# Gated expert rows added to a per-token sum in DRAM, in place of a last stage that gathers them

## The reference

```python
h = layer_norm(ALPHA_RES * h + mix, ln1_g[l], ln1_b[l])            # h1
top_logit, top_e = lax.top_k(logits, TOP_K)                        # TOP_K = 4 of 32
gates = jax.nn.softmax(top_logit, axis=-1)
hu = lax.ragged_dot(xs, w_gate_up, group_sizes) + b_gate_up[e_sorted]
act = (up + 1.0) * gate * jax.nn.sigmoid(SWIGLU_ALPHA * gate)      # gate, up: clipped halves of hu
y = lax.ragged_dot(act, w_down, group_sizes) + b_down[e_sorted]
y = y * g_sorted[:, None].astype(y.dtype)
out = jnp.zeros_like(xf).at[tok].add(y)
h = layer_norm(ALPHA_RES * h + ffn, ln2_g[l], ln2_b[l])
```

## Time and profile before

| | |
|---|---|
| median of 3 runs | 4528.32 us (4526.23 to 4531.88) |
| profiled execution, span | 4529.3 us |
| PE / DVE / ACT / POOL busy | 4289.9 / 3076.1 / 1817.6 / 1010.1 us |
| PE share of the span | 95% |
| DMA | 665.72 MB, 147 GB/s over the span |
| HBM read / written | 543.61 / 120.03 MB |

### The profile page before, as it was taken

One profiled execution on the slowest core, in us unless ns is written; L12 is line 12 of the kernel. 1 busy time (PEld: TensorE's weight loads), 2 busy tenths in 40 slices (PEclk: granted clock), 3 DMA queues, 4 the chain that ended last, 5 costly groups with the idle time before them and its releaser, 6 DMA issues. The chain is left out here.

```text
span 4529.3 us, 70549 instructions
## 1 busy us (share of the span) xinstructions
PE 4289.9 (95%) x24356; PEld 3153.5 (70%) x24356; DVE 3076.1 (68%) x4861; ACT 1817.6 (40%) x2677; POOL 1010.1 (22%) x1152
## 2 busy tenths in 40 slices
PE   8999988999999998699999999999999999999987
PEld 4444434444444454599989889899999999999961
DVE  2587867878888873555556556666676777777768
ACT  1222223443434433233434444444445555555530
POOL 1111101221111122211112212222222222222235
PEclk9999989999999999799999999999999999999986
DMA  6443330120110010544555456474657667667668
GB/s 194 126 122 92 87 101 16 30 27 21 18 23 16 14 27 19 148 158 148 174 168 190 155 183 220 162 250 161 237 197 239 208 230 241 219 234 237 212 214 362
DMA packets 534140, 665.72 MB, mean 147 GB/s; under 512 B 64416, under 2 KB 402592, under 8 KB 533952
## 3 DMA queue, kind: packets, MB, share of 16 engines
q1 hardware_dynamic: 419664, 501.02, 34.7%
q10 hardware_dynamic: 87744, 77.15, 5.4%
q0 software_dynamic: 26576, 85.56, 5.0%
HBM read 543.61 MB, written 120.03 MB: 147 GB/s over the span
## 5 line engine op out<-in xcount | busy, mean ns | idle before, releaser
L2000 PE MATMUL gu<-x_hi,w_hi 128*128 128x240 f32 (+8 forms) x4096 | 1196.5, 292 | 4.1 <-issue 4.1
L2003 PE MATMUL gu<-x_lo,w_hi 128*128 128x240 f32 (+8 forms) x4096 | 1195.5, 292 | 0.5 <-issue 0.5
L2004 PE MATMUL gu<-x_hi,w_lo 128*128 128x240 f32 (+8 forms) x4096 | 1194.1, 292 | 0.0
L2106 DVE TENSOR_TENSOR w_lo<-w_raw,w_hi 128x2048 fp32r<-128x2048 f32 x386 | 874.6, 2287 | 414.1 <-ACT w_hi L2190 386.2
L2190 ACT ACTIVATE w_hi<-w_raw 128x2048 fp32r<-128x2048 f32 x386 | 726.8, 1908 | 207.4 <-PE gu L2004 132.0
L2000 PEld LDWEIGHTS gu<-x_hi,w_hi 128*128 128x128 f32 x4096 | 774.7, 189 | 4.5 <-issue 4.3
L2003 PEld LDWEIGHTS gu<-x_lo,w_hi 128*128 128x128 f32 x4096 | 773.3, 189 | 1.1 <-issue 0.9
L2004 PEld LDWEIGHTS gu<-x_hi,w_lo 128*128 128x128 f32 x4096 | 773.8, 189 | 0.0
L1972 POOL TENSOR_TENSOR a_lo<-up,a_hi 128x384 fp32r<-128x384 f32 x256 | 396.6, 1549 | 1177.8 <-ACT a_hi L2202 1177.8
L570 PE MATMUL proj_acc<-w_in_sb,hT 128*128 128x512 f32 (+1 forms) x1280 | 499.0, 537 | 0.7 <-ACT hT L586 0.7
L2000 PE MATMUL yp<-w_hi,a_hi 128*128 128x512 f32 x1088 | 445.6, 410 | 2.3
(11 more groups left out here) (316 smaller groups left out, 5878.6 us busy)
## 6 DMA issues: line engine op xcount, KB each, us to landing
w_raw<-w_gate_up SPq DMA_DIRECT2D x258, 1024.0 KB, 7.6
w_raw<-w_down SPq DMA_DIRECT2D x128, 1024.0 KB, 8.1
y_dram<-y_rows ACTq DMA_DIRECT2D x128, 256.0 KB, 2.6
y_dram<-zeros ACTq DMA_DIRECT2D x12, 2688.0 KB, 15.5
h_blk<-h_dram SPq DMA_DIRECT2D x32, 512.0 KB, 8.7
qi_dram<-qi_stage ACTq DMA_DIRECT2D x16, 640.0 KB, 3.2
x_in<-x SPq DMA_DIRECT2D x16, 512.0 KB, 6.1
w_in_sb<-w_in SPq DMA_DIRECT2D x4, 2048.0 KB, 14.2
```

The lines of the kernel that those rows point to most:

```text
L2000: op = nc.tensor.matmul(out, s_hi_, m_hi, start=(n == 0), stop=False)
L2003: nc.tensor.matmul(out, s_hi_, m_lo, start=False, stop=False)
L2004: op = nc.tensor.matmul(out, s_lo_, m_hi, start=False, stop=(n == len(pairs) - 1))
L2106: nc.vector.tensor_tensor(w_lo[:, c % 2, cols], raw[:, c % 3, cols], w_hi[:, c % 2, cols].bitcast(F32), ALU.subtract).then_inc(s_lo, 1)
```

## The change

1. A second array in DRAM, `sums`, begins as a copy of h1 (each block is stored twice), and h1 and `sums` get 512 spare rows, cleared to zero. ACT's zero stores into `y` go, and `y` with them.
2. A list entry is now a pair, token number and gate divided by ALPHA_RES (`entry`). Lists are cleared to (2048 + n, 0.0), so that an unused entry names a spare row.
3. In a visit ACT multiplies by the row's gate while it copies out of PSUM. POOL adds each of six tiles to the token's row of `sums` by an indirect DMA with an add (seven DMAs, tile 2 is two). `who` is copied to `who_held` first; `hold_places` and `hold_gates` make row numbers and gates of it behind j = 2 and 3. SP loads the list entries of row tile 2 in its packed form (`load_third`) ahead of the visit.
4. The last stage loads `sums`, adds the bias matmul and norms it, with epsilon divided by ALPHA_RES squared. ACT makes the sums of the rows and of their squares, POOL the scale, DVE three passes. Gathers, `g_sum`, relays of positions and gates go. Eight tiles are in flight.

The core of the diff (row numbers left out; the same names):

```diff
 # attend_stage, SP
-                sp.dma_start(D_["lists"][0:EXPERTS * SEQ, :].rearrange("(p n) o -> p (n o)", p=P),
-                             res[:, 0:EXPERTS * SEQ // P].bitcast(I32)).then_inc(s_clear, 16)
...
+                shape = [CLEARED, 2, 2 * ROWS]
+                sp.dma_start(D_["lists"].rearrange("(p a n) o -> p a (n o)", p=CLEARED, a=2),
+                             res[0:CLEARED, 0:2 * ROWS].bitcast(I32).unsqueeze(1).broadcast_to(shape)
+                             ).then_inc(s_clear, 16)
+                for name in ("h1", "sums"):
+                    sp.dma_start(D_[name][SEQ:, :].rearrange("(m p) n -> p m n", p=P),
+                                 res[:].unsqueeze(1).broadcast_to([P, 1 + ROWS // P, D])).then_inc(s_clear, 16)
...
-                    sp.dma_start(D_["h1"][b * P:(b + 1) * P, :], h1[:]).then_inc(s_h1st, 16)
+                    for name in ("h1", "sums"):
+                        sp.dma_start(D_[name][b * P:(b + 1) * P, :], h1[:]).then_inc(s_h1st, 16)
 # attend_stage, DVE, weigh
-                    nc.vector.tensor_copy(at_i[:], at_f).then_inc(s_at, 1)
+                    nc.vector.tensor_copy(at_i[:], at_f)
+                    nc.vector.tensor_copy(entry[:, :, 0], token[:, b:b + 1].broadcast_to([P, TOP_E]))
...
-                    nc.vector.tensor_scalar(S["gates"][:, b], e_gate, e_inv, None, ALU.mult).then_inc(s_gate, 1)
+                    nc.vector.tensor_scalar(entry[:, :, 1].bitcast(F32), e_gate, e_inv, 1.0 / ALPHA_RES,
+                                            ALU.mult, ALU.mult).then_inc(s_at, 1)
+                    nc.vector.tensor_scalar(S["gates"][:, b], e_gate, e_inv, 1.0 / ALPHA_RES, ALU.mult, ALU.mult
+                                            ).then_inc(s_gate, 1)
 # experts_stage, SP
+                def load_third(v):
...
+                    if not first(v):
+                        sp.wait_ge(s_hold, v)
+                    for i in range(4):
...
+                        sp.dma_start(third[i * FEW:(i + 1) * FEW], D_["lists"][bass.ds(row, FEW), :]
+                                     ).then_inc(s_third, 16)
+                    sp.dma_start(spot[:], A["spots"][bass.ds(rest + few, 1)].rearrange("o p j n -> (o p) j n")
+                                 ).then_inc(s_third, 16)
 
                         if first(v) and c == 0:
                             sp.wait_ge(s_who, 16)
+                            load_third(0)
...
-                        if not first(v) and c in (3, 4):
-                            store_third(v - 1, 2 if c == 3 else 5)
+                        if c == 5:
+                            load_third(v + 1)
 # experts_stage, POOL
+                def hold_places(v):
+
+                    if not first(v):
+                        pool.wait_ge(s_yst[0], 32 * v)
+                        pool.wait_ge(s_yst[1], 32 * v)
+                        pool.wait_ge(s_yst[2], 48 * v)
+                    pool.wait_ge(s_third, 80 * v + 80)
...
+                def scatter(v, n):
+
+                    pool.wait_ge(s_y, 6 * v + n + 3)
+                    nc.gpsimd.tensor_tensor(idle[:, n:n + 1], zero[:, 0:1], zero[:, 0:1], ALU.add)
...
+                    for rows, at, part in parts:
+                        nc.gpsimd.indirect_dma_start(rows, bass.IndirectOffsetOnAxis(ap=at, axis=0), part, None,
+                                                     compute_op=ALU.add).then_inc(s_yst[n % 3], 16)
+
                 def body(v):
+                    list_rows(v + 1)
                     gather(v + 1)
+                    if not first(v):
+                        scatter(v - 1, 5)
                     for j in range(J):
+                        if j == 2:
+                            hold_places(v)
+                        elif j == 3:
+                            hold_gates(v)
                         pool.wait_ge(s_ah, 8 * v + j + 1)
...
+                    for n in range(5):
+                        scatter(v, n)
 # experts_stage, ACT, store
-                    nc.scalar.activation(y[:, slot], yp[:, n % 2], ACT.Copy).then_inc(s_y, 1)
-                    if n % 3 < 2:
...
+                    if n == 0:
+                        act.wait_ge(s_hold, v + 1)
+                    nc.scalar.activation(y[:, slot], yp[:, n % 2], ACT.Copy, scale=gate_now[:, slot:slot + 1]
+                                         ).then_inc(s_y, 1)
 # combine_stage, DVE and ACT
+                def add_bias(t):
...
+                    nc.vector.tensor_tensor(row, row, acc[:, t % SUMS], ALU.add).then_inc(s_tot, 1)
 
                 def finish(t):
...
+                    nc.vector.scalar_tensor_tensor(row, row, column(t, 1), gain[:], ALU.add, ALU.mult)
+                    dve.drain()
                     dve.wait_ge(s_rstd, t + 1)
...
+                    nc.vector.scalar_tensor_tensor(row, row, column(t, 4), bias[:], ALU.mult, ALU.add
+                                                   ).then_inc(s_out, 1)
...
+                def spread(t):
...
+                    nc.scalar.activation(scratch[:, 0], row, ACT.Copy, accum_out=column(t, 0)).then_inc(s_mean, 1)
...
+                    nc.scalar.activation(column(t, 1), column(t, 0), ACT.Copy, scale=-1.0 / D).then_inc(s_mean, 1)
...
+                    nc.scalar.activation(scratch[:, 1], row, ACT.Square, bias=column(t, 1), accum_out=column(t, 2)
+                                         ).then_inc(s_square, 1)
```

More of the change, by code:

```diff
@@ L90, in project_stage @@
     GAPS = 16
-    CLEARS = 12
-    SHARE = (MAX_VISITS - EXPERTS) * ROWS // CLEARS
-    SHARE_N = next(n for n in range(1, SHARE + 1) if SHARE % n == 0 and SHARE // n <= P)
-    assert SHARE * CLEARS == (MAX_VISITS - EXPERTS) * ROWS
     CHUNKS = [(n * BANK, min(BANK, IN_W - n * BANK)) for n in range(5)]
@@ L1821, in experts_stage @@
         a_rest = sb("a_rest", [P, FF // P, REST])
+        third = sb("third", [P, 2], I32)
+        spot = sb("spot", [P, 3, 2], I32)
+        scaled = sb("scaled", [P, 3], I32)
+        at_main = sb("at_main", [P, 2, 2], I32)
+        at_third = sb("at_third", [P, 3], I32)
+        gate_now = sb("gate_now", [P, 3])
+        idle = sb("idle", [P, 6], I32)
         y = sb("y_rows", [P, 3, BANK])
@@ L2176, in _ @@
                 over_visits(dve, body)
+                weigh_experts()
             @block.scalar
@@ L2316, in _ @@
                     sp.wait_ge(s_out, t + 1)
-                    sp.dma_start(out_dram[t * P:(t + 1) * P, :], total[:, t % OUTS]).then_inc(s_st[t % OUTS], 16)
-                for n in range(OUTS):
-                    sp.wait_ge(s_st[n], 16 * len(range(n, TILES, OUTS)))
+                    sp.dma_start(out_dram[t * P:(t + 1) * P, :], total[:, t % AHEAD]).then_inc(s_st[t % AHEAD], 16)
+                    if t >= 1 and t - 1 + AHEAD < TILES:
+                        load(t - 1 + AHEAD)
+                for n in range(AHEAD):
+                    sp.wait_ge(s_st[n], 16 * len(range(n, TILES, AHEAD)))
@@ L2332, in _ @@
                 nc.gpsimd.memset(minus_half[:], -0.5)
[L2333 to L2336 removed]
                 for t in range(TILES):
[L2338 to L2343 removed]
+                    pool.wait_ge(s_square, t + 1)
@@ L2374, in _ @@
+                    op.then_inc(s_bias, 1)
             @block.vector
             def _(dve):
[L2376 to L2381 removed]
@@ L2407, in finish @@
-                def finish(t):
-                    slot = t % OUTS
-                    dve.wait_ge(s_rstd, t + 1)
-                    nc.vector.tensor_scalar(total[:, slot], total[:, slot], small[:, slot, 12:13], small[:, slot, 15:16],
-                                            ALU.subtract, ALU.mult)
-                    dve.drain()
-                    nc.vector.tensor_tensor(total[:, slot], total[:, slot], gain[:], ALU.mult)
-                    dve.drain()
-                    nc.vector.tensor_tensor(total[:, slot], total[:, slot], bias[:], ALU.add).then_inc(s_out, 1)
@@ L2423, in _, with turn @@
+                for t in range(TILES + BEHIND):
+                    if t < TILES:
+                        add_bias(t)
+                    if t == BEHIND:
+                        dve.wait_ge(s_const, 32)
+                    if t >= BEHIND:
+                        finish(t - BEHIND)
             @block.scalar
             def _(act):
-                for g in range(TILES // 4):
+                def turn(g):
                     act.wait_ge(s_bt, g + 1)
@@ L2428, in _ @@
                                          ).then_inc(s_bts, 1)
+                def spread(t):
+                    row = total[:, t % AHEAD]
+                    act.wait_ge(s_tot, t + 1)
+                    nc.scalar.activation(scratch[:, 0], row, ACT.Copy, accum_out=column(t, 0)).then_inc(s_mean, 1)
+                    act.wait_ge(s_mean, 2 * t + 1)
+                    nc.scalar.activation(column(t, 1), column(t, 0), ACT.Copy, scale=-1.0 / D).then_inc(s_mean, 1)
+                    act.wait_ge(s_mean, 2 * t + 2)
+                    wait(act, s_square, t)
```

(6 more changed lines are left out.)

306 lines of the change are left out of this document (111 added, 195 removed).

## The result

| | median us (runs) | ratio to before, 95% interval |
|---|---|---|
| before | 4527.43 (4526.23 to 4531.88) | 1 |
| changed | 4565.14 (4562.89 to 4567.42) | 1.0081 [1.0067, 1.0095] |

What follows compares the result with a forecast made beforehand. PE was taken to bound the expert visits, DMA bytes the last stage. From 4529.3, terms -67.5 (last stage and handover), +3, 0, -0.5 and +1.5 gave 4465.8 on the trace, put at 4464 on the median; range 4448 to 4484.

Steps and rivals of the forecast that it cites:

- The last stage: Final stage after the expert visits: 72.7 us in place of 142.2, VectorE the longest at 3.65 us a tile.
- The rule weighed there: Last stage: VectorE passes with two SBUF inputs block POOL's operations, costing up to 2 us, 4466 in place of 4464.
- The handover: From the last y copy to the last stage: waiting for a scatter's landing, near a plain store's, adds 2 us.
- The start of the experts: First matmul of the experts: load_third(0) ahead of the weights costs 3.3 us, 0.3 kept back, net +3, ends 0 to +7.
- The blocks: Before the experts: VectorE's added operations in attend blocks +1.5 us (0 to +6); zero stores leaving the projection -0.5.
- The visits: The 32 expert visits: added POOL scatters and small operations fit in the slack, 0 us, ends -3 and +10.
- sign of being wrong: Listed among the signs against the forecast: PE idle inside the expert visits.
- Rival 3: Visits: late-landing accumulating scatters hold ScalarE's y copy, then PE; slower than before, 4538 or above; chance 0.04.
- Rival 2: Visits and blocks: scatter, clearing and list work under load cost PE some 0.6 us a visit, 20 us: 4484; chance 0.08.
- The range and the chances: Whole kernel: own bounds 4450 to 4482, range 4448 to 4484; forecast 0.70, faster by over 0.2% 0.95, slower 0.03.

Runs made afterwards that it cites:

- e2: Changed kernel with list copy, drain and load behind j = 4, indices behind j = 7, gathers ahead of tile 4's scatter: 4449.02 us, ratio 0.9826.
- e10: e2 with unused tiles, so that weights' tiles begin at 0 and tiles from x_rows on at 64 modulo 128 bytes: ratio 0.9787.
- e12: Kernel before with unused tiles, weights' tiles at 0 and tiles from x_rows on at 64 modulo 128 bytes: 4496.13 us, ratio 0.9925.
- e8: e2 with unused tiles, weights' tiles at 96 and tiles behind x_rows at 0 modulo 128 bytes: ratio 0.9823.
- e7: Kernel before with two unused tiles, weights' tiles at 96 and x_hi to a_lo at 0 modulo 128 bytes: ratio 0.9954.
- e3: Changed kernel with scatters that overwrite the rows of sums in place of adding to them: 4453.74 us, ratio 0.9829.
- e4: Kernel before with 15 idle fills of 1024 columns, each with a drain, on POOL behind each visit's gathers: 4718.52 us, ratio 1.0415.

## Why the prediction was wrong, step by step

- **The last stage: right.** 71.6 us against 72.7. VectorE's three passes set it, 3.69 us a tile (forecast 3.65); two small errors cancel in part, the third add comes 11.3 us into the stage in place of 13.5, and all behind it takes 1.1 us longer; the groups of the changed kernel's last stage:

```profile
L2386 DVE SCALAR_TENSOR_TENSOR total<-total,small,bias 128x1024 f32<-128x1024 f32 x16 | 20.6, 1284 | 1.2
L2383 DVE SCALAR_TENSOR_TENSOR total<-total,small,gain 128x1024 f32<-128x1024 f32 x16 | 20.4, 1277 | 0.0
...
L2378 DVE TENSOR_TENSOR total<-total,c_acc 128x1024 f32<-128x1024 f32 x16 | 19.4, 1215 | 17.3 <-PE c_acc L2368 14.7 <-DMA total<-sums_dram 2.5
L2412 ACT ACTIVATE scratch<-total,small 128x1024 f32<-128x1024 f32 x16 | 18.4, 1148 | 0.5
```

  ScalarE needs 2.8 us a tile, not 3.4: one of its passes is 1.06. The rule weighed there (VectorE's two-input passes block POOL) cost nothing; POOL's power takes 0.68 us (0.87 before).
- **The handover: too low by 3 us.** +5.1 (from 4.1 us to 9.2) instead of +2. The landing waited for is that of the second of two scatters (issued at 4482.90, landed at 4488.46), and their median landing is 7.3 us. I had put it near that of a plain store.
- **The start of the experts: too high by 2 us.** From the last block's gate to the first product it takes 41.5 us in place of 40.5, +1.0, forecast +3. The five loads and three reads, priced at 3.3, were right: from POOL's first fill behind the barrier to the first product the time grew by 3.5 (29.6 against 26.1). But that fill comes 11.9 us behind the gate in place of 14.4, and of these 2.5 us I had kept 0.3. Counted from the span's start the first product comes 2.8 us later (1883.26 against 1880.48); that this is near 3 is chance.

```profile
1859.55 2.17 SPq L1902 DMA_DIRECT2D third<-lists_dram  x4
1861.93 0.35 SPq L1904 DMA_DIRECT2D spot<-spots  x1
1862.48 14.56 SPq L1885 DMA_DIRECT2D w_raw<-w_gate_up  x6
```

- **The blocks: they cost nothing.** The last block's gate comes at 1841.73 instead of 1839.98, +1.75, where +1.5 less 0.5 was forecast. But 2.6 of it are there at the first gate (779.4 against 776.8), within the 10 us by which that gate differs between profiled executions. From the first gate to the last it takes 1062.3 us in place of 1063.2, so the agreement is luck.
- **The visits: the step that failed.** "I cost the visits at 0, with ends of -3 and +10" was +97.2, and PE was idle inside visits, which the prediction had named as a sign of being wrong: -13.2 mostly by placement, with the mended change's own 3 to 4 us in it (e2's 2394.0 against 2407.2), and +110.4 by the late head (2504.4 against 2394.0). Three things were wrong in it. "The next gathers wait behind scatter 4, 2.5 us later than now" named the wrong starting point: before, the head was released by the transposes behind tile 3 and ran one tile ahead of tile 4's copy, and the step was 13 us. The drain stood in the diff and had no price, though a gap of 6.52 us ahead of a POOL operation behind indirect DMAs could be seen before; such gaps are 3.2 to 6.8 us in these runs. And I asked of the gathers whether they land in time and of a_lo of j = 2 whether it waits, but not what stands behind all of them: a_lo(0), whose lateness goes by `up`'s two slots to VectorE at j = 2 and by gu to PE. Before, POOL's idle time of 8.59 us there was the slack to hold against the sum of the head's additions, which is some 20 us (a_lo(0) 23.2 us behind tile 4's copy, where the gathers had been issued at 2.9); `up`'s two slots gave a narrow visit some 6 us more (17.1 against 11.5), and that wasn't enough either.
- **Rival 3** had the right sign, the wrong mechanism. ScalarE waits for landings 14.3 us in all, 11 times; PE hardly waits for its copies (3.0 us).
- **Rival 2** named "clearing and list work under load" with 0.6 us a visit. That was the right place with a fifth of the size, and no threshold in it.
- **The range and the chances** were also added up wrong, without bearing on the miss: the prediction's own bounds give 4486 or 4487 at the upper end, not 4482, and rival 3, at 0.04, was split into 0.02 and 0.03. Slower than before had 0.03.

## What to carry to other kernels

Where an in-order engine gets more work at one place, add up everything from the event that releases it to the next operation that another engine's buffer waits for, and hold the sum against the idle time ahead of that operation; a drain and a landing count in full. Issue loads for the next round ahead of the work that waits for the slowest event, and take copies and drains where the engine idles anyway. The time beyond the slack is dear where PE is the bound: with idle stretches of about 4 us the granted clock fell as well (6.9 us lost for 4.5 idle). And before a difference of half a per cent is explained by work, compare the matmul's own spacing: a change that resizes tiles can move those behind them, and did here.

The best version of these runs keeps the whole change, has the list, indices and gathers off the head (e2), and the operands placed as in e10: ratio 0.9787 to the kernel before, where the change as it stood gave 1.0081. At equal remainders, e10 against e12 and e8 against e7, the ratios divided give 0.986 and 0.987. By this estimate, across two batches each, the change without its late head is worth what was forecast for it (4464 of 4528, 0.986), and the rest of 0.9787 is placement.

## What the hardware showed that was not expected

- An indirect DMA that adds takes POOL 1.56 us to issue, one that overwrites 0.99, a gather 0.96. In the narrow visits a plain load of the list is waited for 4.5 to 5.3 us behind adding scatters, 1.5 to 1.7 behind overwriting ones and 2.0 to 2.3 in the kernel before. It isn't the adding alone: in the visits of 75 to 87 us it is 4.2 to 4.5, 4.5 to 5.4 and 5.1 to 5.2.
- The 6-element copy of who_held takes 0.20 us in e3 and 2.73 in the changed kernel. There it starts at 3805.44 and VectorE's pass with two SBUF inputs at 3805.84; the copy ends at 3808.17, when the first of two such passes of 2.25 us does:

```profile
3805.84 4.50 DVE L2130 TENSOR_TENSOR w_lo<-w_raw,w_hi 128x2048 fp32r<-128x2048 f32 x2 [5.89 <-ACT w_hi L2217]
```

  The copy's row starts ahead of that pass, but the scatter before it is being issued until 3805.98. In e3 the pass starts at 3767.84, when the copy has ended (3767.61). So half a microsecond in the issue of a scatter became 2.5 us. The Trainium skill (SBUF — State Buffer, "Who interferes with whom") says that such a VectorE instruction blocks a GpSimd instruction that reads SBUF; this pair of rows agrees. Its place was the head of the visits, not the last stage, where the prediction weighed it.
- The visits run 1.4% quicker or slower with where the tiles of the experts stage begin in SBUF (2407.2 against 2373.9 us of visits). Which property of an address decides is open: all four combinations of two remainders modulo 128 were tried, but no remainder modulo 256, and no tile apart from its neighbours.
- The gap on POOL that holds a drain behind indirect DMAs (and little else) is 4.4 us in the changed kernel's median visit (3.2 to 6.2), 4.0 in e3 (3.4 to 6.4) and 5.9 in e4 (3.6 to 6.8). Whether the drain waits for their issue or for their transfers wasn't tried.
